# A gate table filled in two ways: one-hot products for 256 tokens, indirect transfers that add into zeroed DRAM cells for 128

## What is computed

```python
q = (xb @ w_query).reshape(c, PEER_HEADS, 2, HALF_QUERY)
s = jnp.einsum('chpd,pkd->chpk', q, sub_keys)          # two scores tables of 128 keys per head
s_top, i_top = lax.top_k(s, PEER_TOPK)
...
idx = ...                                              # first key * 128 + second key
g = jax.nn.softmax(best, axis=-1)                      # 16 gates per head and token
u = jnp.take(expert_u, idx, axis=0)
act = jax.nn.gelu(jnp.einsum('chkd,cd->chk', u, xb), approximate=False)
vsel = jnp.take(expert_v, idx, axis=0)
return jnp.einsum('chk,chkd->cd', g * act, vsel)
```

## Time and profile before

| | |
|---|---|
| median of 3 runs | 3433.51 us (3433.1 to 3436.86) |
| span of the profiled execution, first to last instruction | 3434.3 us |
| what lies around the span | not given apart; the three runs lie 1.2 below to 2.6 us above the span |
| PE, DVE, ACT, POOL busy | 98%, 77%, 36%, 24% of the span |
| mean granted TensorE clock | 0.997 |
| table stage, first layer | 621.5 to 787 us |
| table stage, second layer | 2315 to 2481.5 us |
| dense stage, first "down" matmul of the first layer | 814.4 us |

### The profile page before, as it was taken

The page is one execution under the profiler, slowest core; times in us unless marked ns, Lnnn a source line. Parts: engine busy times, 40 slices in busy tenths (PEclk is TensorE's granted clock), DMA queues, the critical chain, the costliest instruction groups (busy, mean ns, idle before and its releaser), DMA issues.

```text
span 3434.3 us, 47304 instructions
## 1 busy us (share of the span) xinstructions
PE 3377.4 (98%) x16086; PEld 2755.3 (80%) x16086; DVE 2636.7 (77%) x5503; ACT 1240.8 (36%) x1980; POOL 809.2 (24%) x661
## 2 busy tenths in 40 slices
PE   7999999999999999999999999999999999999998
PEld 4458855898889988888855688559988888898887
DVE  3574389997888888888736734999978888888888
ACT  2333223794223233333214322339833333222332
POOL 0000026002333333333300000440033333333332
PEclk9999999999999999999999999999999999999999
DMA  4313313468888888888741132144698888888885
GB/s 122 104 37 92 119 37 123 161 254 315 319 304 303 305 304 306 306 308 307 259 159 37 37 103 101 44 140 181 246 354 308 309 308 304 302 306 306 304 305 202
DMA packets 270646, 750.58 MB, mean 219 GB/s; under 512 B 19741, under 2 KB 139293, under 8 KB 243904
## 3 DMA queue, kind: packets, MB, share of 16 engines
q1 hardware_dynamic: 196768, 480.57, 39.7%
q0 software_dynamic: 73760, 268.47, 22.7%
HBM read 681.86 MB, written 67.11 MB: 218 GB/s over the span
## 4 chain that ended last, share of the span: by engine, by line
PE 81%; DVE 14%; DMA 2%; POOL 1%; ACT 1%; issue 1%; SPq 0%; DVEq 0%; POOLq 0%; ACTq 0%
PE ps L1239 29%; PE ps L1225 22%; PE ps L1029 7%; PE ps L898 4%; PE ps L1122 4%; DVE OHS L2143 3%; PE ps L1087 3%; PE ps L876 2%; DVE OHS L2139 2%; PE ps L1205 2%; PE ps L1176 2%; DVE URAWL L2109 1%; PE ps L1008 1%; PE ps L843 1%; PE ps L1044 1%
## 5 line engine op out<-in xcount | busy, mean ns | idle before, releaser
L778 POOL DMA_INDIRECT ROWS<-v_rows_dram,GIS x256 | 331.6, 1295 | 576.8 <-DVE X L2213 484.3
L778 POOL DMA_INDIRECT ROWS<-u_rows_dram,GIS x256 | 300.0, 1172 | 610.5 <-DVE STG L2197 536.3
L1578 ACT ACTIVATE AC<-ps 128x384 f32<-128x384 f32 x192 | 94.5, 492 | 927.8 <-PE ps L1225 927.8
L1239 PE MATMUL ps<-VHI,WHI 128*128 128x512 f32 x1536 | 414.5, 391 | 4.8 <-DVE WLO L2178 2.8
L1239 PE MATMUL ps<-VLO,WHI 128*128 128x512 f32 x1536 | 414.8, 392 | 0.0
L1239 PE MATMUL ps<-VHI,WLO 128*128 128x512 f32 x1536 | 412.1, 390 | 0.0
L1571 ACT CAST VHI<-VRAW 128x512 fp32r<-128x512 f32 x512 | 285.6, 619 | 326.9 <-PE ps L1239 325.6
L2213 DVE SCALAR_TENSOR_TENSOR X<-ROWS,STG,X 128x1024 f32<-128x1024 f32 x256 | 328.3, 1282 | 23.0 <-DMA ROWS<-v_rows_dram,GIS 11.1
L1239 PEld LDWEIGHTS ps<-VLO,WHI 128*128 128x128 f32 x1536 | 288.4, 188 | 63.5
L1239 PEld LDWEIGHTS ps<-VHI,WLO 128*128 128x128 f32 x1536 | 289.0, 188 | 62.3
L1239 PEld LDWEIGHTS ps<-VHI,WHI 128*128 128x128 f32 x1536 | 285.6, 188 | 54.1 <-DVE WLO L2178 3.9
(11 more groups left out here) (281 smaller groups left out, 5352.2 us busy)
## 6 DMA issues: line engine op xcount, KB each, us to landing
VRAW<-v_dram SPq DMA_DIRECT2D x128, 1024.0 KB
URAW<-ut_dram SPq DMA_DIRECT2D x128, 512.0 KB, 3.7
URAW<-ut_dram SPq DMA_DIRECT2D x64, 1024.0 KB, 5.6
g_table<-GST SPq DMA_DIRECT2D x12, 4096.0 KB, 12.6
GT<-g_table SPq DMA_DIRECT2D x62, 768.0 KB, 8.1
WR<-w_in_dram SPq DMA_DIRECT2D x8, 2048.0 KB, 12.1
WR<-w_in_dram SPq DMA_DIRECT2D x32, 512.0 KB, 4.7
WR<-w_q_dram SPq DMA_DIRECT2D x8, 2048.0 KB, 8.0
```

What stands on the lines that cost most here:

```text
L778: pool.indirect_dma_start(out=ROWS[:, k % GR, :], out_offset=None, in_=table, in_offset=bass.IndirectOffsetOnAxis(ap=GIS[:, par, k:k + 1], ...
L1239: last = nc.tensor.matmul(ps[:, 2 + o, :], a[:, par, jj, b * P:(b + 1) * P], c[:, dh, jj, :], start=(first and n == 0), stop=(final and n ...
```

## The change

The first of the three dense token blocks no longer goes through the one-hot products. Its 128 tokens own the first two of `g_table`'s six blocks (64 tokens each). In every layer:

- POOL fills a tile `ZERO` with zeros once the mixer's merged output is there, and SP stores it over these two blocks (two stores of 4 MB, after the third query weight tile).
- DVE computes, for each token (partition) and pick, the number of its cell in `g_table` (`table_cells`: four small instructions for heads 0 to 5, once their group is finished, and four for heads 6 and 7 behind the last group). `TBASE` holds each token's part of the number and is made once (`table_base`).
- POOL issues 128 indirect transfers (one per pick number, 8 heads x 16). Each adds one 4-byte gate of every token into its cell. Before each head but the first it waits until all earlier ones have landed, since two heads of a token can pick the same expert.
- The one-hot table stage runs for the other 256 tokens: 32 slots instead of 48. The 136 pieces of early activations are spread over 32 slots (4 or 5 per slot), and SP's list is changed to fit (`LOOP_EARLY` 9, stores at places 4 and 8).
- SP waits for all transfers (`scattered`) after its `load_pair(1, 1)`, and only then loads the first group's gates of the two blocks. DVE's first `weigh` waits for that load too. What stands behind the wait in SP's list waits with it.
- To stay within the number of semaphores, a few are joined (`pre_filter` with `pre_steps`; `dots_done`, `gelu_done`, `gw_ready` in `dot_steps`).

```diff
-TAIL_EARLY, LOOP_EARLY = 14, 6
+TAIL_EARLY, LOOP_EARLY = 14, 9
+TABLE_FROM = P // TOK_IT
+TABLE_ITS = DT // TOK_IT - TABLE_FROM
+TABLE_SLOTS = TABLE_ITS * TOK_IT // OH
+ZERO_RUN = 512
...
+    cells = gd.rearrange("b i j c -> (b i j c)").unsqueeze(1)
...
-    E_SLOTS, E_CHUNKS = DT // OH, KC * (NG - TAIL_EARLY - 1)
+    E_SLOTS, E_CHUNKS = TABLE_SLOTS, KC * (NG - TAIL_EARLY - 1)
...
                     weights([(at_cols(0, KC, 512), cols_of(l, w_q, 512 * i, 512))])
+                    if i == 2:
+                        sp.wait_ge(pool_zeros, 3)
+                        for s in range(2 * TABLE_FROM):
+                            sp.dma_start(gd[s].rearrange("i j c -> i (j c)").rearrange("i (r n) -> i r n", n=ZERO_RUN),
+                                         ZERO[:].unsqueeze(1).to_broadcast([P, NK * CB // ZERO_RUN, ZERO_RUN])
+                                         ).then_inc(zero_stored, 16)
...
-                for it in range(DT // TOK_IT):
-                    if it == DT // TOK_IT - 1:
+                def first_gates(b0, b1):
+                    sp.dma_start(GT0[:, b0:b1].rearrange("p b j c -> p b (j c)"),
+                                 gd[b0:b1, :, 0:JG, :].rearrange("b i j c -> i b (j c)")).then_inc(g_loaded[0], 16)
+
+                sp.wait_ge(zero_stored, 32 * TABLE_FROM)
+                for it in range(TABLE_ITS):
+                    if it == TABLE_ITS - 1:
                         for s in range(2):
                             sp.wait_ge(g_stored[s], 16 * it + 16)
...
+                        first_gates(2 * TABLE_FROM, 2 * (TABLE_FROM + it))
...
-                            if m == (2, 5)[s]:
+                            if m == (4, 8)[s]:
                                 store_gates(it, s)
                         pass_early(TAIL_EARLY + it * LOOP_EARLY + m)
                 load_pair(1, 1)
+                sp.wait_ge(scattered, 16 * PICKS * (l + 1))
+                first_gates(0, 2 * TABLE_FROM)
                 load_v(0, 1)
                 load_one(1, 1)
                 g_all_stored(sp)
...
+                pool.wait_ge(mrg_ready, KC)
+                pool.memset(ZERO[:], 0.0).then_inc(pool_zeros, 1)
...
+                pool.wait_ge(zero_stored, 32 * TABLE_FROM)
+                for h in range(PH):
+                    pool.wait_ge(cells_ready, 1 if h < PH - HG else 2)
+                    if h:
+                        pool.wait_ge(scattered, 16 * (PICKS * l + TOPK * h))
+                    for k in range(TOPK * h, TOPK * (h + 1)):
+                        pool.indirect_dma_start(out=cells, out_offset=bass.IndirectOffsetOnAxis(ap=SCI[:, k:k + 1], axis=0),
+                                                in_=SCW[:, k:k + 1], in_offset=None, compute_op=ALU.add
+                                                ).then_inc(scattered, 16)
...
+                def table_cells(h0, h1):
+
+                    part = slice(TOPK * h0, TOPK * h1)
+                    first, second, weight = (SEL[:, k, 0, h0:h1].rearrange("p h m -> p (h m)") for k in range(3))
+                    dve.wait_ge(sel_ready, h1 // HG)
+                    nc.vector.tensor_copy(SCW[:, part], weight)
+                    st.did(nc.vector.scalar_tensor_tensor(GIF[:, part], first, float(NK), second, ALU.mult, ALU.add))
+                    st.then(dve)
+                    st.did(nc.vector.tensor_scalar(GIF[:, part], GIF[:, part], float(CB), TBASE, ALU.mult, ALU.add))
+                    st.then(dve)
+                    nc.vector.tensor_copy(SCI[:, part], GIF[:, part]).then_inc(cells_ready, 1)
...
                         finish_group(i - 1)
+                    if i == NGRP - 1:
+                        table_cells(0, PH - HG)
...
                 finish_group(NGRP - 1)
+                table_cells(PH - HG, PH)
...
-                    dve.wait_ge(g_loaded[par], use * 16)
+                    dve.wait_ge(g_loaded[par], use * 16 + 16 * (1 - par))
```

More of the change, by code:

```diff
@@ L98 @@
 DT = DB * P
+TABLE_FROM = P // TOK_IT
+TABLE_ITS = DT // TOK_IT - TABLE_FROM
+TABLE_SLOTS = TABLE_ITS * TOK_IT // OH
+TABLE_BANKS = TABLE_ITS * TOK_IT // 4
+ZERO_RUN = 512
 NOUT = 2 * DB
@@ L324, in encoder @@
     WF1, _ = sb("WF1", [P, DT])
+    SCI, _ = sb("SCI", [P, PICKS], I32, offset=preb_at + 8 * DT)
+    SCW, _ = sb("SCW", [P, PICKS], offset=preb_at + 8 * DT + 4 * PICKS)
+    ZERO, _ = sb("ZERO", [P, ZERO_RUN], offset=preb_at)
+    assert 2 * PICKS <= DT and ZERO_RUN <= 2 * DT and end_d <= preb_at
     NEGG, _ = sb("NEGG", [P, TOK_IT])
@@ L364, in encoder @@
     rows_loaded = [sem(f"rows_loaded{i}") for i in range(GR)]
+    scattered = sem("scattered")
     ROWS_LAYER = 16 * 2 * PICKS // GR
@@ L404, in encoder @@
     oh_act = lsem("oh_act")
+    zero_stored = lsem("zero_stored")
+    cells_ready = lsem("cells_ready")
     before_late = len(layer_sems)
@@ L450, in g_all_stored @@
         for s in halves:
-            e.wait_ge(g_stored[s], 16 * (DT // TOK_IT) + 16)
+            e.wait_ge(g_stored[s], 16 * TABLE_ITS + 16)
     def early_slot(e):
@@ L481, in late_sems_clear @@
             e.wait_ge(next_layer, l)
-    SINCOS_ARGS, NORM_STEPS, LAST = 15, 6, DEPTH - 1
+    SINCOS_ARGS, NORM_STEPS, LAST = 22, 6, DEPTH - 1
     FINAL_ORDER = (NB - 1, 0, 1, 2)
@@ L1184, in _ @@
                 pe.wait_ge(sel_ready, NGRP)
-                for b in range(DB):
+                for b in range(1, DB):
                     for i in range(3):
@@ L1212, in _ @@
                     early_parts(NG - 1, k)
-                pe.wait_ge(g_bank_free, DT // 4 + GBANKS)
+                pe.wait_ge(g_bank_free, TABLE_BANKS + GBANKS)
                 pe.nop().then_inc(v_out, 1)
@@ L1503, in _ @@
                     early_act(e, e)
-                for b in range(DB):
-                    act.wait_ge(sel_turned, b + 1)
+                for b in range(1, DB):
+                    act.wait_ge(sel_turned, b)
                     nc.scalar.copy(IDXT[:, :, b * P:(b + 1) * P],
@@ L1608, in _ @@
                     step(it, 1)
-                act.wait_ge(dots_done, GSTEPS)
-                nc.scalar.activation(DOT[:], DOT[:], ACT.Gelu).then_inc(gelu_done, 1)
+                act.wait_ge(dot_steps, GSTEPS)
+                nc.scalar.activation(DOT[:], DOT[:], ACT.Gelu).then_inc(dot_steps, 1)
                 with act.Fori(GSTEPS // 2, (NG - 2) // 2) as it:
@@ L1688, in sine_arguments @@
                 assert pre.n == SINCOS_ARGS
-            fil = Steps(pre_filter)
+            fil = pre
             def filter_angles():
@@ L1702, in filter_angles @@
                         sine_arguments()
+                table_base()
                 dve.wait_ge(dec_loaded, 64)
@@ L1773, in ffn_scales, with table_base @@
                     scale_block(XS2, b)
+            def table_base():
+                dve.wait_ge(first_loads, 16)
+                pre.did(nc.vector.tensor_tensor_reduce(FK[:, 0:P], ident, iota, 1.0, 0.0, ALU.mult, ALU.add, accum_out=TBASE))
+                pre.then(dve)
+                pre.did(nc.vector.tensor_scalar(TFAR, TBASE, float(CB), float(P * NK * CB - CB), ALU.is_ge, ALU.mult))
+                pre.then(dve)
+                pre.did(nc.vector.tensor_tensor(TBASE, TBASE, TFAR, ALU.add))
+                pre.then(dve)
             dve.wait_ge(x_here[DVE_SQUARE], 16)
@@ L1884, in _ @@
                     kb_done.append(total)
-                dve.wait_ge(pads_zero, 2)
+                dve.wait_ge(pool_zeros, 2)
                 dve.wait_ge(hs_stored, 16)
@@ L2115, in _ @@
                 nc.vector.tensor_copy(GG[:], picks[2])
+                dve.wait_ge(cells_ready, 2)
                 st.did(nc.vector.scalar_tensor_tensor(GIF[:], picks[0], float(NK), picks[1], ALU.mult, ALU.add))
@@ L2201, in keep_dots @@
                     dve.wait_ge(rows_used, s * GS + (GR + GS))
-                    nc.vector.tensor_copy(DOT[:, bass.ds(s * GS, GS)], STG[:, par, :]).then_inc(dots_done, 1)
+                    nc.vector.tensor_copy(DOT[:, bass.ds(s * GS, GS)], STG[:, par, :]).then_inc(dot_steps, 1)
                 def stage_weights(s, par):
@@ L2266, in _ @@
                     step(it, 1, rows=dot)
-                dve.wait_ge(gelu_done, 1)
-                nc.vector.tensor_tensor(GW[:], DOT[:], GG[:], ALU.mult).then_inc(gw_ready, 1)
-                dve.wait_ge(gw_ready, 1)
+                dve.wait_ge(dot_steps, GSTEPS + 1)
+                nc.vector.tensor_tensor(GW[:], DOT[:], GG[:], ALU.mult).then_inc(dot_steps, 1)
+                dve.wait_ge(dot_steps, GSTEPS + 2)
                 with dve.Fori(GSTEPS // 2, (NG - 2) // 2) as it:
```

19 lines of the change are left out of this document (9 added, 10 removed).

## The result

The changed kernel takes 3625.87 us (median of 4, 3622.91 to 3631.15) against 3434.4 for the kernel before: a ratio of 1.056, 95% interval 1.055 to 1.058. It is 5.6% slower. The forecast was 3448, with a range up to 3565; the result lies outside it. The profiled execution has a span of 3629.3 us, 195.0 above that of before.

The account below looks back on a forecast made before the run. PE work was taken to bound the kernel end to end. A 31 us saving against a wait of about 40 for the last transfer gave +7 us per layer, +14 on 3434.3: 3448 us on the median, range 3378 to 3565.

Parts of the forecast that it names:

- the landmark: PE's first "down" matmul, at 814.4 in the first layer; each us it moves is a us of the layer.
- The rule that a layer changes by the landing of the last transfer less 798.5: At SP's wait for the gates: the layer changes by last landing minus 798.5, by no less than -27 us.
- I take 1.08: POOL's transfers: 1.08 us per instruction, estimated from gathers, plus a 0.30 gap; 128 of them take 176.6 us.
- The upper end, 1.96: POOL's transfers: longest gather, 1.96 us, as upper end per instruction; with the 0.30 gap, 289 us for 128.
- The sign that I gave for a dear add: Single POOL transfer rows above 1.6 us would show that DVE or the adding is dear.
- The landings: POOL's eight waits for landing, 2.5 us each, 20 in all, plus 6 us for meetings with 4 MB stores.
- The floor: Table stage with transfers hidden: 31.2 us of PE saved, 2.0 added, some 2 given back; -27 us per layer.
- My own sign for a prediction wrong in kind: PE's table stage itself being longer than 140 us would make the prediction wrong in kind.
- The rival that the bound does not fall: Table stage would not shorten if ACT or DVE lost step with PE; hidden under transfers, no chance of its own.
- Hidden transfers: POOL's transfers lose the gap, pitch 0.94 to 1.15 us, SP never waits; 3380 us, chance 0.24.
- Slow landings and dearer instructions: POOL's transfers at 1.33 + 0.30 us, landings 49 us; +62.5 us per layer, 3559 us, chance 0.20.
- DVE shuts POOL out: Each POOL transfer waits for a DVE instruction, 2.45 us each; +144.5 us per layer, 3723 us, chance 0.06.

Follow-up runs that it names:

- run 1: Changed kernel with all 128 transfers writing their word in place of adding it; 3466.15 us, ratio 1.0098 to the kernel before.
- run 6: Changed kernel with a separate cell for each pick number and no POOL waits between heads; 3569.62 us.
- run 7: Changed kernel redivided: 64 tokens by 64 adding transfers, 320 by one-hot products in 40 slots, everything computed; 3438.91 us, ratio 1.0021 to the kernel before.
- run 3: Changed kernel with only the 64 transfers of heads 0 to 3; 3412.00 us.
- Run 2: Changed kernel with each transfer replaced by a no-operation, the 32 slots and waits kept; 3402.11 us.
- run 9: Changed kernel without transfers, ACT's splits 2 slots ahead in place of 3 and DVE's half of each split one slot later; 3369.28 us.
- Run 12: The kernel before with only DVE's half of the splits moved one slot later; 3430.70 us, ratio 0.9995.
- run 10: Changed kernel redivided: 64 tokens by transfers in two alternating sets of 32, lists packed by POOL, DVE kept waiting for the second packing; 3587.24 us.
- run 4: Changed kernel with 128 transfers of 64 words in place of 128 words; 3598.57 us.
- run 11: The two-set division with POOL's packed lists in tiles of their own, DVE not waiting, and both split slot numbers moved; 3432.08 us, ratio 0.9995.

## Why the prediction was wrong

**What held.** The stage, the landmark and the rule between them. The rule that a layer changes by the landing of the last transfer less 798.5 gives, with the gates' load issued at 898.2 as the landing, +99.7 a layer; 97.3 were measured, since the way from there to the first "down" took 13.5 us and not 15.9. By the same rule run 1 is +18.8 (16.9 measured) and run 6 +72.7 (137.4 for the two layers measured, 68.7 each). POOL began at 602.5 (603.2 forecast), the gap before a transfer was 0.30 but for three holes, the zeros show no cost, PE's one-hots took 65.2 us (62 forecast), and the hole in PE was where it was said to be. A hole of 117 us where 40 to 50 were expected is the miss.

**The step that failed: "I take 1.08".** The sum for POOL was 128 x 1.08 = 138.2 us of instructions; they took 218.8. These 80.6 us are most of the 92 by which the last landing came late (898.2 against 806); POOL's gaps add 13.5 (below), and the landings and the start took 1.7 off. The price had two parts, a bare 0.94 and 0.14 for DVE. The first was wrong: adding costs 0.58 us per transfer over writing (1.54 against 0.96), 74 us a layer. The second came out near in the sum by luck: 218.8 less 128 x 1.54 is 21.7 us, 0.17 per transfer (0.14 forecast), but nearly all of it falls on the transfers up to 787, where the mean is 0.28 above the bare price, and those behind ran beside a DVE at rest because the chain was so long. I had looked for the price of short pieces and of a DRAM destination, and run 1 shows that I was right to add nothing for them; the operation itself I had only as "a DMA engine reads the cell and then writes it", a matter of the engines and not of POOL's instruction. The upper end, 1.96, was there, but I weighed the range by gathers, and no row of a gather says anything about an add. What the sum priced was in fact the kernel with plain writes: there the instructions took 146.4, the gates' load went out at 817.25 (806 forecast), and the median was 3466 (3448 forecast), inside the range. The sign that I gave for a dear add, single rows above 1.6 us, was badly placed too: a bare adding row has 1.54.

**The landings** were sized well: 23.6 us for seven and 1.4 for the last, against 20 + 6, and run 6 gains about as much without them (27 us). They were not a fixed price, though: in the second layer the seven took 27.8, and in the first layer of run 7 the same kind of wait took 51 us behind 4 MB stores.

**What was not in the sum.** One hole of 12 us in each layer has no releaser in the trace:

```profile
744.72 0.43 SPq L665 DMA_DIRECT2D g_table<-GST  x1
```

```profile
758.17 1.54 POOL L799 DMA_INDIRECT g_table<-SCW,SCI  x1 [12.25 <-issue]
```

The transfer starts 13.5 us after SP issued a 4 MB store. In the second layer it is 12.23 us, 13.4 after the store of 2538.05; run 3 has the same hole in both layers, runs 1 and 6 have none. With two holes of about 2 us near the end, the first layer's gaps come to 51.9 us where the sum had 128 x 0.30 = 38.4. What stopped POOL there was not tested.

**The floor was wrong too, under cover.** I wrote that "both engines then have over 10 us to spare", and gave the floor as -27 us a layer. Run 2 gives -15. My own sign for a prediction wrong in kind, PE's table stage longer than 140 us, came true: from 627.06 to the end of the piece at 775.43 it was 149 us, and 133 in run 9. The rival that the bound does not fall, because ACT or DVE loses step, was about half true, and it was rightly said to be hidden under the transfers. Run 9 gives the reason: with 9 early activations in 16 slots, DVE reaches its half of a split before ACT has made its own, waits 27 us, and falls behind PE. One slot later it does not, and the layer falls by 31.7, about the 31.2 of PE's products and more than the floor. Run 12 shows no gain from the same number at 6 activations in 16 slots; in the kernel before, DVE waited only 1.3 us there for ACT's half.

**The rivals.** *Hidden transfers* did not come: the gap stayed. *Slow landings and dearer instructions*, 3559, was the right kind with the wrong term; its instruction was 1.33 and the landings its main price. *DVE shuts POOL out* put +144.5 on a layer with 2.45 us per transfer, for a reason that does not carry it: with DVE at rest the instruction still takes 1.55 (run 10). Only beside DVE's 128x2048 instructions do a few transfers keep its pace (last section). The Trainium skill (SBUF — State Buffer, SBUF: two separate sides) has a factor of five for a GpSimd DMA beside a VectorE copy in a two-port mode; the trace shows the direction, 1.82 against 1.54 beside the table stage, and not the size. The fixed cost of about 2.0 us per GpSimd DMA in the Trainium skill (DMA: Bandwidth & Descriptors, Anatomy of one DMA) agrees with the holes that met no store, 2.1 to 2.3 us.

## What to carry to other kernels

A transfer that adds has another price than one that writes: look for a row of the same operation before you price 128 of them, and where there is none, let the range cover a doubling. Count instructions, not words: half the words in as many transfers saved an eighth of what half the transfers saved, so pack lists until every partition works, write where nothing is there yet, and let two independent sets cover each other's landings. When a stage gets fewer slots for the same side work, move the places written for the old ratio as well: here one slot number was worth 30 us.

## What the runs showed of the hardware

- With DVE at rest, an indirect transfer from POOL that adds takes 1.54 us for 128 addresses (changed kernel) and 1.41 for 64 (run 4); one that writes takes 0.96 (run 1). The gap before each is 0.30 to 0.31 where nothing holds it.
- An adding transfer is recorded as more packets: the software queue held 36864 more than before (256 transfers, 144 each), and with plain writes 8192 (32 each).
- Beside DVE's instructions of 128x2048 (2.2 to 2.3 us each), adding and writing transfers take the same time. The fourth and fifth transfer of the first layer, first in run 1 and then in the changed kernel:

```profile
607.62 1.90 POOL L799 DMA_INDIRECT g_table<-SCW,SCI  x1 [0.30 <-issue]
609.82 2.02 POOL L799 DMA_INDIRECT g_table<-SCW,SCI  x1 [0.30 <-issue]
```

```profile
610.47 2.02 POOL L799 DMA_INDIRECT g_table<-SCW,SCI  x1 [0.30 <-issue]
612.78 1.90 POOL L799 DMA_INDIRECT g_table<-SCW,SCI  x1 [0.30 <-issue]
```

The pitch of 2.2 to 2.3 is that of DVE's instructions. In the changed kernel DVE starts such instructions at 608.77 and 613.30, in run 1 at 608.72 and 613.25; the transfer under way then ends 1.39 and 1.38 us later where it adds, 0.80 and 0.79 where it writes. So it looks as if each had waited for DVE and then done its own work; this was read from the rows and not tested by itself.
- POOL's small copies are hit harder than its transfers. Eight copies of 32x8 words took 5.34 us beside DVE's table work (run 11, second packing) and 1.75 with DVE at rest (run 10, second packing):

```profile
738.66 5.34 POOL L802 COPY SCW<-WGT 32x8 f32<-32x8 f32 x8
```

```profile
706.22 1.75 POOL L800 COPY SCW<-SEL 32x8 f32<-32x8 f32 x8
```

- In the hole the granted clock fell to 0.50 (1.2 GHz) and stayed there while PE did nothing; eight matmuls that took 1.55 us ahead of it took 2.93 right behind it, and the clock was at 1.00 from 910 on. Against a hole of 117 us that is small.
